# A mixture-of-experts layer: expert weight chunks of 512 columns of the gate or of the up half in turn, loaded by half chunks

## What is computed

```python
x = x + moe_ffn(rms_norm(x, moe_norm_w), ...)        # top 4 of 32, softmax over the chosen logits

def expert_block(idx, e):                            # idx: tokens of expert e
    xb = hf[idx]
    gu = xb @ w_gu[e] + b_gu[e]                      # (tokens, 1024) @ (1024, 2048), float32
    gate = minimum(gu[:, :1024], 7.0)
    up = clip(gu[:, 1024:], -7.0, 7.0)
    act = (up + 1.0) * (gate * sigmoid(1.702 * gate))
    return act @ w_down[e] + b_down[e]               # (tokens, 1024) @ (1024, 1024)
```

## Time and profile before

| | us |
|---|---|
| three runs, median | 2340.07 |
| three runs, lowest and highest | 2331.64, 2341.68 |
| the profiled execution | 2335.18 |
| span of its instructions on the core | 2333.5 |
| of it: before the first superblock | 741.9 |
| of it: 15 wide superblocks | 856.3 |
| of it: 17 narrow superblocks | 643.7 |
| of it: after the last superblock's products | 91.6 |

### The profile page before, as it was taken

The page is one execution under the profiler, slowest core; times in us unless marked ns, Lnnn a source line. Parts: engine busy times, 40 slices in busy tenths (PEclk is TensorE's granted clock), DMA queues, the critical chain, the costliest instruction groups (busy, mean ns, idle before and its releaser), DMA issues. The chain is left out here.

```text
span 2333.5 us, 36367 instructions
## 1 busy us (share of the span) xinstructions
PE 2135.3 (92%) x11267; PEld 1816.4 (78%) x11268; DVE 1588.6 (68%) x1927; ACT 1290.0 (55%) x1703; POOL 503.4 (22%) x621
## 2 busy tenths in 40 slices
PE   7999998898994999999999999999999999999950
PEld 5877777655884899878998898998777998798940
DVE  4446654622337678888778877778888778878748
ACT  4254433444223566666666766666767667766630
POOL 2015762233001111111111111111212111211124
PEclk9999997898996999999999999999999999999975
DMA  4234554403245679899779978879999879989768
GB/s 154 90 97 108 138 171 147 172 5 107 109 160 169 223 253 313 294 359 327 243 252 309 359 248 281 281 254 340 357 363 357 286 256 342 354 295 310 250 236 352
DMA packets 435708, 567.03 MB, mean 243 GB/s; under 512 B 28400, under 2 KB 328433, under 8 KB 435657
## 3 DMA queue, kind: packets, MB, share of 16 engines
q1 hardware_dynamic: 423657, 523.64, 68.7%
q0 software_dynamic: 12000, 42.74, 5.1%
HBM read 506.98 MB, written 57.51 MB: 242 GB/s over the span
## 5 line engine op out<-in xcount | busy, mean ns | idle before, releaser
L1567 DVE TENSOR_TENSOR VL<-RAW,VH 128x2048 fp32r<-128x2048 f32 x389 | 886.6, 2287 | 146.7 <-ACT VH L1562 146.4
L1562 ACT ACTIVATE VH<-RAW 128x2048 fp32r<-128x2048 f32 x390 | 725.8, 1907 | 87.1 <-DMA RAW<-in_expert_w_gate_up 52.2
L2294 PE MATMUL banks<-T,VH 128*128 128x384 f32 x1920 | 550.6, 361 | 12.6 <-ACT yb L2087 5.7
L2296 PE MATMUL banks<-T,VL 128*128 128x192 f32 x1680 | 422.3, 251 | 0.0
L2294 PEld LDWEIGHTS banks<-T,VH 128*128 128x128 f32 x1920 | 355.1, 189 | 16.3 <-issue 12.4
L2296 PEld LDWEIGHTS banks<-T,VL 128*128 128x128 f32 x1680 | 322.8, 192 | 0.2
L207 PE MATMUL banks<-VH,A 128*128 128x512 f32 x512 | 209.0, 408 | 6.7 <-DVE A L2133 6.5
L208 PE MATMUL banks<-VL,T 128*128 128x512 f32 x544 | 212.2, 390 | 0.0
L209 PE MATMUL banks<-VH,T 128*128 128x512 f32 x544 | 212.2, 390 | 0.0
L207 PE MATMUL banks<-VH,T 128*128 128x512 f32 x544 | 212.0, 390 | 0.0
L209 PE MATMUL banks<-VH,A 128*128 128x512 f32 x512 | 200.5, 392 | 0.0
(11 more groups left out here) (356 smaller groups left out, 3646.2 us busy)
## 6 DMA issues: line engine op xcount, KB each, us to landing
RAW<-in_expert_w_gate_up SPq DMA_DIRECT2D x264, 1024.0 KB, 7.7
RAW<-in_expert_w_down SPq DMA_DIRECT2D x130, 1024.0 KB, 9.6
RW<-in_w_in SPq DMA_DIRECT2D x24, 512.0 KB, 5.6
dY<-zeros SPq DMA_DIRECT2D x17, 512.0 KB, 7.5
dY<-yb SPq DMA_DIRECT2D x68, 128.0 KB, 9.2
dY<-yb SPq DMA_DIRECT2D x32, 256.0 KB, 10.2
xin<-in_x SPq DMA_DIRECT2D x8, 512.0 KB, 10.6
MBC<-dM SPq DMA_DIRECT2D x8, 512.0 KB, 10.7
```

Source lines behind the costliest of these rows:

```text
L1562: act.activation(VH[:, i, ks], RAW[:, i, ks], ACT.Copy).then_inc(s_hi, 1)
L1567: dve.tensor_tensor(VL[:, i, ks], RAW[:, i, ks], VH[:, i, ks].bitcast(f32), ALU.subtract).then_inc(s_w, 1)
L2294: last = pe.matmul(o[:, 0:2 * NW], VH[:, c % 3, k, col], T2[:, k], start=k == 0, stop=k == KT - 1)
L2296: pe.matmul(o[:, HI_ALL], VL[:, c % 3, k, col], T2[:, k, HI_ALL], start=False, stop=False)
```

## The change

A gate/up chunk is now 512 columns of gate or of up alone: chunk 0 is gate columns 0 to 511, chunk 1 the up columns 0 to 511, chunk 2 the other gate columns, chunk 3 the other up columns. All rows that the weight DMAs read are then 2 KB. `load` is two `load_half`, each two DMAs of 512 KB for one half of the k-tiles; SyncE issues the second half of chunk c + 5 when VectorE has split the second half of chunk c + 2, and the first half of chunk c + 6 when it has split the first half of chunk c + 3. ScalarE waits for each half by itself.

In the narrow body gate and product come once per two chunks, over 512 columns. In the wide body the 16 column blocks n of 128 columns (4 gate, 4 up, 4 gate, 4 up) are evicted one by one from a ring of four banks; the Silu of a gate block waits in `sg` until its up block comes. `pick(n)` gives (a, g, j): which pair of chunks, gate 0 or up 1, which block in the chunk. The table of biases follows.

```diff
+    def load_half(sp, c, e, hf):
+        for g in range(2):
+            ks = slice(hf * HK + 2 * g, hf * HK + 2 * g + 2)
+            if c < GU:
+                at = (c % 2) * D + (c // 2) * CH
+                src = w_gu[bass.ds(e, 1), :, ks, at:at + CH]
+            else:
+                src = w_dn[bass.ds(e, 1), :, ks, (c - GU) * CH:(c - GU + 1) * CH]
+            sp.dma_start(RAW[:, c % 3, ks], src.rearrange("a p k n -> p (a k) n")).then_inc(s_raw[c % 3][hf], 16)
     def load(sp, c, e):
-        for g in range(2):
-            if c < GU:
-                dst = RAW[:, c % 3, :, g * HC:(g + 1) * HC]
-                src = w_gu[bass.ds(e, 1), :, :, g * D + c * HC:g * D + (c + 1) * HC]
...
+        load_half(sp, c, e, 0)
+        load_half(sp, c, e, 1)
...
@@ SyncE, both bodies @@
                     for c in range(NCH):
                         wait(s_w, s * N2 + (2 * (c + 2) + 2))
-                        load(sp, (c + 5) % NCH, e if c == 0 else en)
+                        load_half(sp, (c + 5) % NCH, e if c == 0 else en, 1)
...
+                        wait(s_w, s * N2 + (2 * (c + 3) + 1))
+                        load_half(sp, c, en, 0)
...
@@ ScalarE, both bodies @@
                 def round_next(s, c, late=None):
...
+                    act.wait_ge(s_raw[c % 3][0], s * 64 + 32 * ((c + 3) // 3 + 1))
                     split_hi(act, c % 3, 0)
                     if late is not None:
                         late()
+                    act.wait_ge(s_raw[c % 3][1], s * 64 + 32 * ((c + 3) // 3 + 1))
                     split_hi(act, c % 3, 1)
...
@@ ScalarE, wide; GN = 16 @@
+                    for n in range(GN):
+                        a, g, j = pick(n)
+                        i, at = 4 * a + j, (n % 2) * NW
+                        act.wait_ge(s_mm, s * N4 + (n + 1))
+                        if n >= 2:
+                            act.wait_ge(s_up, s * GN + (n - 1))
+                        act.activation(lo2[:, at:at + NW], ps[n % 4][:, NW:2 * NW], ACT.Identity, bias=bcur[:, g, i:i + 1]).then_inc(s_ea, 1)
+                        if g == 0:
+                            if n == 8:
+                                block_hi(s, 3)
+                            act.wait_ge(s_up, s * GN + (n + 1))
+                            act.activation(sg[:, j * NW:(j + 1) * NW], zz[:, n % 2], ACT.Silu, scale=ALPHA).then_inc(s_sg, 1)
+                        elif j >= 1:
+                            block_hi(s, i - 1)
+                        if n == GN - 1:
+                            block_hi(s, i)
+                        if j == 3:
+                            round_next(s, n // 4)
...
@@ VectorE, narrow @@
                     for c in range(NCH):
...
+                        if c == GU - 1:
+                            act_lo(s, 0)
+                        if c < GU and c % 2 == 1:
+                            dve.wait_ge(s_mm, s * N4 + (4 * c + 4))
...
+                            dve.tensor_scalar(u1[:], ps[2], LIMIT + 1.0, 1.0 - LIMIT, ALU.min, ALU.max).then_inc(s_up, 8)
...
+                            dve.scalar_tensor_tensor(out=qa[:], in0=sg[:, 0:CH], scalar=TOP, in1=u1[:], op0=ALU.min, op1=ALU.mult).then_inc(s_a, 4)
+                        second_half(s, c)
+                        if c == GU - 1:
+                            act_lo(s, 1)
                         first_half(s, c)
...
@@ VectorE, wide @@
+                    for n in range(GN):
+                        a, g, j = pick(n)
...
+                        dve.tensor_tensor(zz[:, n % 2, HI[0]], ps[n % 4][:, HI[0]], lo2[:, at + UN:at + NW], ALU.add)
+                        dve.tensor_tensor(zz[:, n % 2, HI[1]], ps[n % 4][:, HI[1]], lo2[:, at:at + UN], ALU.add).then_inc(s_up, 1)
+                        if n == 8:
+                            block_lo(s, 3)
+                        if g == 1:
+                            if j >= 1:
+                                block_lo(s, i - 1)
+                            dve.wait_ge(s_clip, s * G2 + (i + 1))
...
+                        if n == GN - 1:
+                            block_lo(s, i)
+                        if j == 1:
+                            second_half(s, n // 4)
+                        if j == 3:
+                            first_half(s, n // 4)
...
@@ TensorE, narrow @@
                         elif c == GU:
+                            pe.wait_ge(s_act, s * G2 + (2 + HK))
+                            product(s, o, c, A2, range(HK - 1))
+                            turned(s, 1)
+                            product(s, o, c, A2, [HK - 1])
+                            tokens(0, s * 16 + 32, s * 2 + 2)
                             pe.wait_ge(s_act, s * G2 + (2 + G2))
+                            product(s, o, c, A2, range(HK, KT)).then_inc(s_mm, 4)
...
@@ TensorE, wide @@
+                    for n in range(GN):
+                        a, g, j = pick(n)
+                        c, o = n // 4, ps[n % 4]
...
+                        if n >= 4:
+                            pe.wait_ge(s_up, s * GN + (n - 3))
```

More of the change, by code:

```diff
@@ L1515, in layer_kernel @@
     VL = r6.take("VL", [P, 3, KT, CH], f32r)
-    lo2 = r6.take("lo2", [P, 2, 2, NW])
-    zz = r6.take("zz", [P, 2, 2, NW])
-    u1 = r6.take("u1", [P, 2, HC])
+    lo2 = r6.take("lo2", [P, CH])
+    zz = r6.take("zz", [P, 2, NW])
+    u1 = r6.take("u1", [P, CH])
+    qa = r6.take("qa", [P, CH])
     r6e = Region(ext.at, nc.sbuf_usable_end - ext.at)
@@ L1524, in layer_kernel @@
     r6t = Region(A_TR, 4 * KB)
-    sg = r6t.take("sg", [P, 2, HC])
-    qa = r6t.take("qa", [P, 2, HC])
+    sg = r6t.take("sg", [P, GU * NW])
     xg = r6e.take("xg", [P, 2, D])
@@ L1682, in _ @@
                 act.wait_ge(s_wlo, 4)
-                act.wait_ge(s_raw[0], 32)
-                split_hi(act, 0, 0)
-                split_hi(act, 0, 1)
+                for hf in range(2):
+                    act.wait_ge(s_raw[0][hf], 32)
+                    split_hi(act, 0, hf)
                 for t in range(TT):
@@ L1705, in _ @@
                 for c in (1, 2):
-                    act.wait_ge(s_raw[c], 32)
-                    split_hi(act, c, 0)
-                    split_hi(act, c, 1)
+                    for hf in range(2):
+                        act.wait_ge(s_raw[c][hf], 32)
+                        split_hi(act, c, hf)
             @block.vector
@@ L1991, in _ @@
                     load(sp, c + 3, 0)
+                sp.wait_ge(s_w, 5)
+                load_half(sp, 5, 0, 0)
                 n = superblocks(sp, narrow, wide)
                 for i in range(3):
-                    wait(s_raw[i], n * 64 + (64 if i < 2 else 32))
+                    for hf in range(2):
+                        wait(s_raw[i][hf], n * 64 + (64 if i < 2 or hf == 0 else 32))
                 for i in range(2):
@@ L2235, in bias_in, with turned @@
                     return pe.matmul(o, hot_e[:, c // 2], btab[:, (c % 2) * CH:(c % 2 + 1) * CH], start=True, stop=False)
[L2237 to L2243 removed]
+                def turned(s, a):
+                    pe.wait_ge(s_a, s * G2 + (2 + (a + 1) * 4))
+                    pe.wait_ge(s_act, s * G2 + (2 + a * 4))
+                    for j in range(4):
+                        last = pe.transpose(ps[4 + a][:, j * P:(j + 1) * P], qa[:, j * P:(j + 1) * P], ident[:])
+                    last.then_inc(s_aT, 4)
                 def begin(s):
@@ L2312, in wide @@
                             last = product(s, o, c, A2, range(KT))
-                        last.then_inc(s_mm, 1)
+                        last.then_inc(s_mm, 2)
                         o = ps[2 * (c % 2) + 1]
-                        left_product(o, c, range(KT)).then_inc(s_mm, 1)
+                        left_product(o, c, range(KT)).then_inc(s_mm, 2)
                 tokens(0, 16)
```

205 lines of the change are left out of this document (76 added, 129 removed).

## The result

| | us |
|---|---|
| before, median of 4 runs (lowest, highest) | 2340.1 (2331.6, 2341.7) |
| after, median of 4 runs (lowest, highest) | 2367.2 (2367.2, 2369.0) |
| ratio, 95% interval | 1.0128 [1.0111, 1.0145] |

The account below looks back on a forecast made before the run. TensorE was taken to bound all but six narrow superblocks, where the full DMA queue does. Wide +28.5, narrow -19.8 and outside nothing sum to +8.7, giving 2343.9 or 2348.8 by baseline; 2346 us was predicted, range 2328 to 2366.

Parts of the forecast that it names:

- Wide, the mechanism: Wide superblocks: TensorE waits 1.7 us for VectorE's last low part in chunk 4; +1.9 each, fifteen +28.5 us.
- matmuls of gate and up: Wide, TensorE: more neighbouring matmuls with the same matrix part (VL-VL, VH-VH) cost +0.2 us per superblock.
- `zz` pair: Wide evictions: the clamps of 128 and 64 columns cost 0.28 and 0.21, less 0.08 overlap: 0.41 us.
- an up block on VectorE: Wide evictions: `zz` 0.41, GpSimd 0.67 and `qa` 0.27 make 1.35 us per up block.
- Narrow: Narrow superblocks: 36.7 us each, above the DMA's 36.2; seventeen take 623.9 against 643.7, -19.8 us (-28 to -11).
- The start wait: Narrow superblock's start: TensorE's 0.61 us wait for the next tokens' low part on VectorE goes.
- The 36.2 of own work: Narrow, TensorE: 148 matmuls at 33.6 plus 2.6 for transposes and the first matmuls behind them, 36.2 us.
- the upper bound that the step gave: Narrow superblock: at most 37.2 us, with a wait of 0.4 and the old 0.6 at the start.
- The DMA: Narrow runs: full DMA queue sets the pace; 2-KB rows at 388 GB/s give 36.2 us; half loads change no byte.
- The third rival: Narrow runs: DMA does not gain, six superblocks stay at 38.8, eleven save 0.7; +21, 2358 us; chance 0.12.
- Outside: nothing: Outside the superblocks: the stage before loads and rounds the same first chunks, so no time changes.
- The second rival: Wide: ScalarE-VectorE exchange costs more; `zz` at 0.52 adds 1.2 per superblock, 18 us: 2364; chance 0.20.

Follow-up runs that it names:

- the run without it: Changed kernel, narrow body: VectorE makes the first product's low part ahead of the third chunk's second weight split; 2365.8 us, 1.0122, narrow 37.2.
- the best order: Changed kernel, narrow body: both products' low parts and the next tokens' low part each moved ahead of a weight split on VectorE; 2366.1 us, narrow 36.6.
- the last version: Changed kernel with wide split and ScalarE copy reordered, SyncE's sixth-chunk load moved to its next round, narrow low parts ahead of splits; 2316.9 us, 0.9915.

## Why the prediction was right and wrong

**Wide, the mechanism: right; the size: +1.9 predicted, +2.6 measured.** By its steps, from the superblock's start:

| step | predicted | measured |
|---|---|---|
| matmuls of gate and up | +0.2 | -0.18 (36.35 against 36.53) |
| rounding starts | 10.6, 21.4, 31.1, 43.3 | 10.7, 21.6, 31.4, 43.9 |
| `zz` pair | 0.41 | 0.41 |
| an up block on VectorE | 1.35 | 1.42 |
| wait for chunk 4's bank | none | 0.46 |
| TensorE asks for the last low part | 42.3 | 42.4 |
| it is ready | 44.0 | 44.6 |

So 0.46 + 2.3 of waits less 0.18 make 2.6. Two terms failed. One is the up block, taken as 1.35. The other is chunk 4's bank: the step had TensorE start chunk 4 at 37.5 without a wait, and named a wait for a drained bank only inside gate and up. GpSimd's row for the block whose `zz` ends at 1177.23 starts 0.35 us behind it, not 0.29 as in the earlier trace rows:

```profile
1177.58 0.35 POOL L2050 TENSOR_SCALAR u<-zz 128x192 f32<-128x192 f32 x1 [3.27 <-DVE zz L2200]
```

The earlier trace rows show one block; both delays occur in both kernels, and over all 120 such blocks the median is 0.29 us before and 0.35 after. Why they differ is not shown. Of the 0.6 us by which the low part came late, the table has 0.3 up to the third rounding start (most of it in the three up blocks of chunk 1) and 0.3 in the four up blocks of chunk 3, 0.07 each. The own work was mis-sized by its sign: the extra same-matrix neighbours cost nothing that can be seen, and that saving hid a part of the other two misses.

**Narrow: right in kind, 8.4 us too hopeful.** The start wait went, and the clamp and product took 0.69 each. The superblock of after that starts at 1254.37, VectorE and then TensorE:

```profile
1276.85 0.68 DVE L2154 SCALAR_TENSOR_TENSOR A<-banks,A 128x512 fp32r<-128x512 f32 x1
...
1281.58 0.68 DVE L2154 SCALAR_TENSOR_TENSOR A<-banks,A 128x512 fp32r<-128x512 f32 x1
```
```profile
1277.77 0.49 PE L207 MATMUL banks<-VH,A 128*128 128x512 f32 x1
...
1282.40 0.49 PE L207 MATMUL banks<-VH,A 128*128 128x512 f32 x1 [0.28 <-DVE A L2154]
```

The second low part is ready 27.9 us after the start, where 27.8 was predicted. TensorE takes it up at 28.0, and what is left takes 9.2 (to 1291.57), where the sum had 36.7 - 27.8 = 8.9. These 0.5 us are the miss: the 0.14 from VectorE to TensorE, which I left out, and the matmuls behind transposes and waits. The 36.2 of own work were also added up short: 24 transposes at 0.1 and four matmuls behind them at 0.1 more are 2.8, not 2.6. There was also a wait that the step didn't name: chunk 4 starts at 1277.77, right behind the first low part (ends 1277.53) and 0.47 after the matmul before it, instead of 0.23. It cost nothing, since the second low part would not have come earlier, as the run without it showed. With the best order 27.5 + 9.1 = 36.6 are left. The measured 37.2 is the upper bound that the step gave, but by luck: its bound kept the old start wait, which went.

**The DMA: the outcome right, the cause half.** "There the DMA queue is full" holds, and 2-KB rows lift the limit: 370 to 379 GB/s and no waits, and up to 384 in the last version, whose superblocks take 36.6 us. But I gave half loads no worth ("changes no byte"), while alone they bring 8.4 us with runs this short: a lead in time is as good as a rate as long as it lasts. The third rival is excluded by the runs with 2-KB rows. The size rule of the Trainium skill ("DMA: Bandwidth & Descriptors", Specifications), full rate from 512 B, does not hold here: 361 GB/s with 1-KB rows at a full queue, up to 384 with 2-KB rows while the queue still keeps up.

**"Outside: nothing" was wrong**, by 3.5 us. The step looked at the stage before alone. SyncE's queue was read for what it delays in the loop, not for when it leaves it.

**The sum.** +8.7 was forecast; the three misses are +9.5 (wide), +8.4 (narrow) and +3.5 (end), all to one side. Without any one of them the time would lie inside the range. The second rival (slower, 2364) came nearest, with its mechanism "the exchange costs more", though not through `zz`, which cost the 0.41 of the forecast. That its time is so near is chance: it asked for 18 us more in the wide superblocks and nothing in the narrow ones or at the end. What the forecast lacked most was the thought that the wait is an order and not a price: where the step laid out "split to 40.1; two up blocks, the last `qa` from 42.6", it named the split whose move was worth 30 us.

## What to carry to other kernels

Look at what stands in front of the low part, the copy or the flag that the bound engine waits for: a split of 2.2 us ahead of it was most of the loss in the wide body. Moving it behind brought the change from 1.3% slower to the time of the kernel before, and moving the copy too made it 0.5% faster. Moving one such step may only move the wait to the next step of the same queue, or into the next block, as in the narrow body; lay out the whole queue for a period before saying what is gained. When an edit moves a load to a later point of an engine's loop, ask also when that engine leaves the loop.

## What the runs showed of the hardware

A round of SyncE's loop that does nothing costs 0.69 us and one of VectorE's 0.72, so 21 of them put 15 us between the last superblock and the next stage in both kernels. The engine that leaves last sets the time: VectorE before the change, SyncE after it. A DMA queue at its limit (361 GB/s with 1-KB rows) is not seen at once in TensorE's time: with loads issued by halves four narrow superblocks, 150 us, passed before the first one that took longer.
